# Decay levels of a gated linear attention beside the input projection of a two-block network, a folded Fourier transform, and four PSUM banks in turn

## The chip, the cores and the metric

The kernel runs on one core of a Trainium2 chip, as one launch that computes the whole network. The metric is device time in microseconds (us), the median of the runs of a kernel. The engines are TensorE (PE in the rows, its weight loads PEld), VectorE (DVE), ScalarE (ACT), GpSimd (POOL) and SyncE (SP), which issues the DMAs. Each engine takes its instructions in order, and semaphores tie the engines together.

## The reference, cut to what matters

Two blocks of two layers each over 512 tokens of width 1024, all in float32. The second block has 256 more context tokens in its first layer, so 768 in all. In block 1 each layer is a mixer, a layer norm, a convolutional feed-forward and another layer norm. The change touches mostly the first mixer of block 2:

```
p = h @ w_in                                  # 1024 -> 2064
u_f, q, k, v, r, z = split(p)                 # 512, 256, 256, 512, 512, 16
loga[d] = log_sigmoid(z @ w_gate[d] + b_gate[d]) / 16     # d: forward, backward
# per chunk, for each direction, b = cumsum(loga):
attn[i, j] = sum_d q[i, d] k[j, d] exp(b[i, d] - b[j, d]),  j <= i
o = attn @ v + (q * exp(b)) @ S
S = exp(b_last) * S + (k * exp(b_last - b))^T v
o = (o_f + o_b) * rsqrt(mean(o^2) + eps) * g * silu(r)
f = fft2(u_f, over time and over 128 features of each of 4 groups, ortho).real
y = concat(f, o) @ w_out
```

## The kernel before

Activations lie with features on the 128 partitions and tokens along the free axis. A weight product `pe_product` (line 317) takes a tile of 128 outputs; its weight and its input are each split into a high and a low part of the fast float32 format, so each of the 8 parts of 128 inputs takes three matmuls per token segment (512 latent tokens, and 256 of context where they take part). The order of all tiles is one list; tile g uses weight buffer g % 2. SyncE loads the tile, ScalarE makes its high part (`act_split`, line 287) once product g − 2 is done, VectorE its low part (`dve_split`, line 295), and TensorE multiplies. The product goes to PSUM banks 2(g % 2) and 2(g % 2) + 1, for the context and the latent segment, and may start when tile g − 2 has been taken from there. Where only latent tokens take part, bank 2(g % 2) stays unused. `pe_pair` (line 343) runs the first two tiles of a stage staggered, as their inputs come out of a norm part by part.

In the feed-forward of block 1 (`act_ffn`, `dve_ffn`, `dve_up`) ScalarE takes the middle tap of the convolution from PSUM, VectorE adds the other two (line 1615), and only then is the bank free. Ahead of that, `act_norm` ends with eight scalings of `x` (`act_scaled`, line 1439), which the residual needs later.

The second block's mixer runs in four steps, one after the other on every engine:

- `in2`: 17 tiles (k and q, r, z, v, u by their places in the stacked weight), each copied out by ScalarE (line 355).
- `pe_fourier`: the gates (line 2186) of both directions, with ScalarE and VectorE making log-sigmoid and the running sums (`dve_gl_gates`); the values turned by TensorE transposes (line 2052); then for four groups the feature transform (line 2065), ScalarE's copy of its rows, and the time transform (line 2078) with 4 + 4 row tiles of 128 for latent tokens and 2 + 2 for context.
- the levels: for chunks of 128 tokens, the lower triangle of scores is built from the diagonal and 7 halvings, for two directions: 15 score steps. Step i has arguments by VectorE (`dve_decay_arg`, lines 671 and 672, two halves), an exp by ScalarE (line 678), a multiplication with q and k by VectorE (`dve_decayed`, line 687, two halves), 24 small products by TensorE (`pe_scores`, line 771), and a copy of the wanted places out of PSUM by VectorE (`dve_scores`, line 798). Steps 0, 1, 2, 8 and 9 are "wide" (128 columns a product, three groups of units, the third in the banks of the first); the others "narrow" (64 columns, two groups). Masks for the copies are cast by GpSimd (line 735) from a DMA.
- the tail: keys with their decay turned (line 2284), state products (line 2306) and VectorE's chain of states (line 2491), attention times values (line 2329), q times states (line 2344), a norm per head, then the gate `silu(r)`.

After that comes `out2`, which starts as a pair with the Fourier groups' high and low parts.

## Time and profile before

| what | us |
|---|---|
| median of 3 runs | 2865.52 |
| lowest and highest run | 2852.60, 2868.56 |
| profiled execution | 2854.13 |
| its span | 2852.8 |
| TensorE busy | 2641.2 (93%) |
| VectorE busy | 1745.5 (61%) |
| ScalarE busy | 1083.6 (38%) |

The profile is one execution. Matmuls are pipelined and their ends modelled, so that a busy TensorE need not be at its peak. A float32 matmul outside the weight products leaves two records of each kind. "Granted clock" is the share of full speed that TensorE was allowed. Times in the rows are from the start of the span.

### The profile page before, as it was taken

The page shows a single profiled execution, that of the slowest core. Times are in us where ns is not written, and L with a number is a line of the kernel's source. Part 1 is how long each engine was busy: PE and PEld are TensorE (multiplying, and loading weights), DVE is VectorE, ACT ScalarE, POOL GpSimd, SP SyncE. Part 2 cuts the span into 40 slices and gives each one's busy share as a digit, 9 for nine tenths or more (in the row PEclk, how much of TensorE's full clock was granted, in tenths as well). Part 3 has the DMA queues.
Part 4 walks back from the last instruction along what each step waited for, and adds up shares of the span by engine and source line. Part 5 has one row for each costly group of instructions (what it writes and reads, how often), then busy time and mean ns, then how long its engine had stood idle before and what let it go on. Part 6 is the DMA issues. An engine that isn't in the chain of part 4 may idle for free.

```text
span 2852.8 us, 32720 instructions
## 1 busy us (share of the span) xinstructions
PE 2641.2 (93%) x13412; PEld 2207.7 (77%) x13412; DVE 1745.5 (61%) x2381; ACT 1083.6 (38%) x1472; POOL 37.5 (1%) x38
## 2 busy tenths in 40 slices
PE   5987889999989999899888999999999887999998
PEld 4766768888768888688587788888887666788887
DVE  6786588787778877611595555335533676564464
ACT  2434453233453244422334433213324454443342
POOL 0010000000100000000100000000000000000000
PEclk9986999999999999999859999999999999999999
DMA  8620358755235666231000122211211100233332
GB/s 316 217 81 1 103 165 277 237 177 167 70 101 184 200 201 201 65 112 52 10 1 30 46 67 66 71 57 60 73 64 51 37 29 9 73 97 104 89 105 80
DMA packets 79700, 295.60 MB, mean 104 GB/s; under 512 B 8752, under 2 KB 10416, under 8 KB 79296
## 3 DMA queue, kind: packets, MB, share of 16 engines
q1 hardware_dynamic: 79552, 293.52, 31.9%
q8 instruction: 106, 1.74, 0.2%
q14 instruction: 42, 0.34, 0.0%
HBM read 291.39 MB, written 2.10 MB: 103 GB/s over the span
## 4 chain that ended last, share of the span: by engine, by line
PE 83%; DVE 9%; ACT 4%; issue 1%; POOL 0%; DMA 0%; DVEq 0%; ACTq 0%; SPq 0%
PE ps L317 69%; PE ps L343 3%; PE ps L771 2%; PE ps L2669 1%; PE ps L2078 1%; PE ps L2637 1%; DVE gatt L798 1%; DVE p_lo L2939 1%; DVE w_lo L295 1%; DVE anm L2921 1%; PE ps L1679 1%; DVE h_lo L525 1%; PE ps L1120 1%; ACT h_hi L519 0%; ACT sq L1902 0%
## 5 line engine op out<-in xcount | busy, mean ns | idle before, releaser
L317 PE MATMUL ps<-h_hi,w_hi 128*128 128x512 f32 (+1 forms) x2400 | 807.2, 372 | 24.3 <-DVE conv_u L1615 10.4
L317 PE MATMUL ps<-h_hi,w_lo 128*128 128x512 f32 (+1 forms) x2400 | 798.4, 368 | 0.0
L317 PE MATMUL ps<-h_lo,w_hi 128*128 128x512 f32 (+1 forms) x2400 | 796.7, 367 | 0.0
L295 DVE TENSOR_TENSOR w_lo<-w_raw,w_hi 128x1024 fp32r<-128x1024 f32 (+2 forms) x319 | 413.9, 1298 | 559.8 <-ACT w_hi L287 558.9
L287 ACT ACTIVATE w_hi<-w_raw 128x1024 fp32r<-128x1024 f32 (+2 forms) x319 | 356.7, 1118 | 864.3 <-PE ps L317 833.9
L317 PEld LDWEIGHTS ps<-h_hi,w_hi 128*128 128x128 f32 x2400 | 453.2, 189 | 108.2 <-issue 20.7
L317 PEld LDWEIGHTS ps<-h_lo,w_hi 128*128 128x128 f32 x2400 | 453.6, 189 | 77.3 <-issue 2.9
L317 PEld LDWEIGHTS ps<-h_hi,w_lo 128*128 128x128 f32 x2400 | 452.8, 189 | 75.8
L317 PE MATMUL ps<-g_hi,w_hi 128*128 128x512 f32 (+1 forms) x880 | 295.7, 369 | 0.8 <-DVE w_lo L295 0.8
L317 PE MATMUL ps<-g_lo,w_hi 128*128 128x512 f32 (+1 forms) x880 | 294.8, 368 | 0.0
L317 PE MATMUL ps<-g_hi,w_lo 128*128 128x512 f32 (+1 forms) x880 | 294.8, 368 | 0.0
L439 DVE CUSTOM_DVE_ANT_0 m_raw<-m_raw,c_act,small 128x1024 f32<-128x1024 f32 x179 | 226.3, 1279 | 1.3 <-DMA m_raw<-in_ada_w 1.3
L364 DVE SCALAR_TENSOR_TENSOR x<-ps,mods,x 128x512 f32<-128x512 f32 (+1 forms) x112 | 75.3, 690 | 197.8 <-PE ps L317 190.0
L317 PEld LDWEIGHTS ps<-g_hi,w_hi 128*128 128x128 f32 x880 | 165.3, 188 | 29.6 <-DVE w_lo L295 1.4
L317 PEld LDWEIGHTS ps<-g_lo,w_hi 128*128 128x128 f32 x880 | 165.3, 188 | 28.2 <-issue 0.5
L317 PEld LDWEIGHTS ps<-g_hi,w_lo 128*128 128x128 f32 x880 | 165.3, 188 | 27.8
L1615 DVE SCALAR_TENSOR_TENSOR conv_u<-ps,small,conv_u 128x510 f32<-128x510 f32 (+2 forms) x220 | 148.5, 691 | 3.1
L1571 ACT ACTIVATE g_hi<-gated 128x512 fp32r<-128x512 f32 (+1 forms) x88 | 60.3, 686 | 223.7 <-DVE gated L1628 223.7
L1566 ACT ACTIVATE silu_u<-conv_u 128x512 f32<-128x512 f32 (+1 forms) x88 | 60.4, 687 | 191.7 <-DVE conv_u L1615 191.7
L343 PE MATMUL ps<-h_hi,w_hi 128*128 128x256 f32 (+1 forms) x192 | 66.6, 402 | 59.4 <-DVE w_lo L295 34.6
L1630 DVE TENSOR_TENSOR g_lo<-gated,g_hi 128x512 fp32r<-128x512 f32 (+1 forms) x88 | 66.8, 759 | 66.2 <-ACT g_hi L1571 66.2
L343 PEld LDWEIGHTS ps<-h_hi,w_hi 128*128 128x128 f32 x192 | 37.8, 204 | 76.4 <-issue 52.9
(396 smaller groups left out, 2824.5 us busy)
## 6 DMA issues: line engine op xcount, KB each, us to landing
w_raw<-in_up SPq DMA_DIRECT2D x176, 512.0 KB, 3.6
m_raw<-in_w_mod SPq DMA_DIRECT2D x96, 512.0 KB, 3.7
w_raw<-in_down SPq DMA_DIRECT2D x64, 704.0 KB, 4.1
m_raw<-in_ada_w SPq DMA_DIRECT2D x83, 512.0 KB, 4.7
w_raw<-in_in SPq DMA_DIRECT2D x39, 512.0 KB, 3.7
w_raw<-in_out SPq DMA_DIRECT2D x16, 512.0 KB, 3.6
m_start<-in_ada_w SPq DMA_DIRECT2D x13, 512.0 KB, 12.1
w_raw<-in_qkv SPq DMA_DIRECT2D x12, 512.0 KB, 3.6
```

Of the source, the lines that this page charges most:

```text
L287: act.activation(k.w_hi[s][:, 0:w], k.w_raw[s][:, 0:w], ACT.Copy).then_inc(*k.tick("w_hi", g))
L295: dve.tensor_tensor(k.w_lo[s][:, 0:w], k.w_raw[s][:, 0:w], k.w_hi[s][:, 0:w].bitcast(F32), ALU.subtract).then_inc(*k.tick("w_lo", g))
L317: last = pe.matmul(ps[:, bank, 0:tn], a[:, c, :], b[:, c, t0:t0 + tn], start=c == 0 and n == 0, stop=c == kt - 1 and n == 2)
L343: last = pe.matmul(ps[:, bank, 0:tn], a, b[:, c, t0:t0 + tn], start=c == 0 and n == 0, stop=c == KD - 1 and n == 2)
L364: last = dve.scalar_tensor_tensor(x, k.ps[:, 2 * s + bank, 0:tn], gates[bank], x, ALU.mult, ALU.add)
L439: dve.tensor_tensor_reduce(w, w, k.c_act[:, last, :], 1.0, bias, ALU.mult, ALU.add, column(last)).then_inc(*k.tick("mods", job.key))
L525: k.nc.vector.tensor_tensor(k.h_lo[:, f, ts], value, k.h_hi[:, f, ts].bitcast(F32), ALU.subtract).then_inc(*k.tick("h_lo", key))
L771: last = pe.matmul(out, lhs[rows, cols], right, start=True, stop=True)
L1566: act.activation(f["silu"][:, :], f["conv"][0][:, :], ACT.Silu).then_inc(*k.tick("silu", g))
L1571: act.activation(f["hi"][:, j, :], f["g"][:, :], ACT.Copy).then_inc(*k.tick("g_hi", (block, layer, half, j)))
L1615: last = dve.scalar_tensor_tensor(o, ps[:, bank, lo - d:hi - d], w, o, ALU.mult, ALU.add)
L1630: dve.tensor_tensor(f["lo"][:, j, :], f["g"][:, :], f["hi"][:, j, :].bitcast(F32), ALU.subtract).then_inc(*k.tick("g_lo", key))
```

## The change

**Banks.** For the stages with latent tokens alone (`out1`, the feed-forwards of block 1, the last feed-forward of block 2) tile g uses one bank of (1, 3, 0, 2)[g % 4] and waits for the taking of tile g − 4. **Scalings.** `act_scaled` leaves `act_norm`, and runs one at a tile, from tile 4 of the following up projection. **Order of `in2`.** The tiles are now z, k and q, u, v, r. The gates come inside tile 2 and behind it; the score steps come one after every fifth part, from the fifth part of tile 5 on; the turning of one direction's keys at the third part of tile 16. VectorE's and ScalarE's work for them stands between their splits of the tiles. Buffers lie in other places, and the load of the masks and GpSimd's part come at the start of `in2`. **Fourier.** VectorE folds each group's tokens in `in2` (sum and difference of token t and its mirror), so that the time transform has half of the rows; the tables are half as large, and loaded after the last product of `in2`. High and low halves are made from PSUM directly. The rest is reordered between value turning, keys, states and groups. `silu(r)` and its two table loads stand between the Fourier copies.

```diff
+def in_four(g):
+    return ORDER[g][0] in ("out1", "up00", "down00", "up01", "down01", "up11", "down11")
+def product_bank(g, bank):
+    return (1, 3, 0, 2)[g % 4] if in_four(g) else 2 * (g % 2) + bank
+def bank_release(g):
+    before = g - 4 if in_four(g) else g - 2
+    return (RELEASE[before],) if before >= 0 else ()
...
-    ps = k.ps[:, 2 * s:2 * s + 2, :] if place is None else k.ps[:, place - 1:place + 1, :]
     if 0 in part:
         pe.wait_ge(*k.seen("w_lo", g))
-        for key in free or ((RELEASE[g - 2],) if g >= 2 else ()):
+        for key in free or bank_release(g):
...
+                last = pe.matmul(k.ps[:, product_bank(g, bank) if place is None else place, 0:tn], a[:, c, :], b[:, c, t0:t0 + tn],
...
-    for f in range(KD if split is not None else 0):
-        act_scaled(k, which, f)
...
+            if not half and scaled is not None and 4 <= n < 4 + KD:
+                act_scaled(k, scaled, n - 4)
...
+Z, QK, U, V, R = 0, 1, 5, 9, 13
+LEVEL_STEPS = {4 + 5 * i: i for i in range(2 * LEVELS + 1)}
+KEYS_STEP = 90
...
     sp.wait_ge(*k.seen("h_lo", (("rms", 0), KD - 1)))
-    sp.dma_start(k.tmp[0][0:16, :].rearrange("p (f c) -> p f c", c=P), k.ins["w_gate"]).then_inc(*k.tick("turn_load", "gate", 16))
+    sp.dma_start(k.mean[0:16, :].rearrange("p (f c) -> p f c", c=P), k.ins["w_gate"]).then_inc(*k.tick("turn_load", "gate", 16))
+    sp.dma_start(k.rstd[:, :], k.ins["reset2"]).then_inc(*k.tick("turn_load", "reset2", 16))
+    sp.dma_start(mask_stage(k.gkdt[1], 2), k.ins["masks2"]).then_inc(*k.tick("load", "masks2", 16))
+    sp_tiles(k, BASE["in2"] + 3, 14)
+    sp.wait_ge(*k.seen("product", BASE["in2"] + 16))
     sp.dma_start(k.feat[:, :], k.ins["dft_f"]).then_inc(*k.tick("load", "dft_f", 16))
-    sp.dma_start(k.dlat[:, :, :, :], k.ins["dft_lat"]).then_inc(*k.tick("load", "dft_lat", 16))
-    sp.dma_start(k.dctx[:, :, :, :], k.ins["dft_ctx"]).then_inc(*k.tick("load", "dft", 16))
-    sp.dma_start(k.greset, k.ins["reset2"]).then_inc(*k.tick("load", "reset2", 16))
-    sp_tiles(k, BASE["in2"] + 3, 14)
+    sp.dma_start(k.dctx[:, :, :, :], k.ins["dft_ctx"]).then_inc(*k.tick("load", "dft_ctx", 16))
+    sp.dma_start(k.dlat[:, :, :, :], k.ins["dft_lat"]).then_inc(*k.tick("load", "dft", 16))
...
 def pe_in2(k):
-    pe_pair(k, BASE["in2"], TALL, k.h_hi, k.h_lo, rms_ready(0))
-    for n in range(2, 17):
-        pe_product(k, BASE["in2"] + n, TALL, k.h_hi, k.h_lo)
+    g0 = BASE["in2"]
+    pe_pair(k, g0, TALL, k.h_hi, k.h_lo, rms_ready(0))
+    pe_product(k, g0 + 2, TALL, k.h_hi, k.h_lo, part=range(0, 4))
+    pe_gl_gates(k, 0)
+    pe_product(k, g0 + 2, TALL, k.h_hi, k.h_lo, part=range(4, KD))
+    pe_gl_gates(k, 1)
+    for n in range(3, U):
+        pe_product(k, g0 + n, TALL, k.h_hi, k.h_lo)
+    for n in range(U, 17):
+        for c in range(KD):
+            pe_product(k, g0 + n, TALL, k.h_hi, k.h_lo, part=range(c, c + 1))
+            step = (n - U) * KD + c
+            if step in LEVEL_STEPS:
+                pe_gl_scores(k, LEVEL_STEPS[step])
+            if step == KEYS_STEP:
+                pe_gl_keys(k, 1)
 def act_in2(k):
-    for n in range(17):
-        if n:
+    for n in range(1, 18):
+        if n < 17:
             act_split(k, BASE["in2"] + n + 1)
-        if n:
-            act_keep_in2(k, n - 1)
-    act_keep_in2(k, 16)
-def act_keep_in2(k, n):
-    act_keep(k, BASE["in2"] + n, k.z2[:, n, :] if n < 9 else k.more[:, n - 9, :], TALL)
+        act_keep(k, BASE["in2"] + n - 1, in2_place(k, n - 1), TALL)
+        if n == 2:
+            act_gl_biased(k, 0)
+        if n == 3:
+            act_gl_exp(k, 0)
+            act_gl_log(k, 0)
+            act_gl_biased(k, 1)
+        if n == 4:
+            act_gl_exp(k, 1)
+            act_gl_log(k, 1)
+        if n == U:
+            act_decay(k, "g", 0, gl_combs(k)[0], 1.0 / 16.0)
+        for i in levels_beside(n):
+            if i + 1 < len(GL_STEPS):
+                act_decay(k, "g", i + 1, gl_combs(k)[(i + 1) % 3], 1.0 / 16.0)
+        if n == 15:
+            act_gl_decays(k)
+        if n == 17:
+            act_gl_turned(k, 1)
...
 def dve_in2(k):
     for n in range(1, 17):
         dve_split(k, BASE["in2"] + n + 1)
+        if n == 2:
+            dve_gl_abs(k, 0)
+        if n == 3:
+            dve_gl_gates(k, 0)
+            dve_gl_abs(k, 1)
+        if n == 4:
+            dve_gl_scaled(k)
+            dve_gl_gates(k, 1)
+        if n == U:
+            dve_gl_first(k)
+        for i in levels_beside(n):
+            dve_gl_level(k, i)
+        if U + 2 <= n < U + 6:
+            dve_fo_fold(k, n - U - 2)
+        if n == 15:
+            dve_gl_decays(k)
+def dve_fo_fold(k, g):
+    dve, u = k.nc.vector, k.fu[:, g, :]
+    dve.wait_ge(*k.seen("kept", BASE["in2"] + U + g))
+    for n, (t0, tn, _) in enumerate(FOLDED):
+        half = tn // 2
+        right = u[:, t0 + half + 1:t0 + tn]
+        dve.tensor_tensor(right, right, u[:, t0 + half - 1:t0:-1], ALU.subtract).then_inc(*k.tick("unfolded", (g, n)))
+    for n, (t0, tn, _) in enumerate(FOLDED):
+        half = tn // 2
+        left = u[:, t0 + 1:t0 + half]
+        dve.wait_ge(*k.seen("unfolded", (g, n)))
+        last = dve.scalar_tensor_tensor(left, left, 2.0, u[:, t0 + tn - 1:t0 + half:-1], ALU.mult, ALU.add)
+    last.then_inc(*k.tick("folded", g))
...
-    pe_gl_gates(k, 0)
     pe_fo_values(k)
+    pe_gl_keys(k, 0)
+    pe_gl_add(k, 1)
     pe_fo_features(k, 0)
-    pe_gl_gates(k, 1)
-    for g in range(4):
-        if g + 1 < 4:
-            pe_fo_features(k, g + 1)
-        pe_fo_time(k, g)
+    pe_fo_features(k, 1)
+    pe_fo_time(k, 0)
+    pe_fo_features(k, 2)
+    pe_fo_time(k, 1)
+    pe_gl_add(k, 0)
+    pe_fo_features(k, 3)
+    pe_fo_time(k, 2)
+    pe_fo_time(k, 3)
...
+    pe.wait_ge(*k.seen("kept", BASE["in2"] + V + 3))
+    pe.wait_ge(*k.seen("turned_out", ("gkd", 1, 2)))
+    pe.wait_ge(*k.seen("att", ("g", steps, len(score_groups(GL_STEPS, steps, 24)) - 1)))
...
-    for t in range(TALL // P):
-        last = pe.matmul(k.ps[:, 4 + t // 2, (t % 2) * 256:(t % 2) * 256 + 256], k.more[:, 4 + g, t * P:(t + 1) * P], k.feat[:, :],
-                         start=True, stop=True)
+    pe.wait_ge(*k.seen("folded", g))
+    for t0, tn, odd in FOLDED:
+        for j in range(tn // 2 // P):
+            t = odd // P + j
+            place = lambda rows, part: k.ps[rows, t // 2, (t % 2) * 256 + part * P:(t % 2) * 256 + (part + 1) * P]
+            middle = t0 + tn // 2
+            pe.matmul(place(slice(0, P), 0), u[:, t0 + j * P:t0 + (j + 1) * P], k.feat[:, 0:P], start=True, stop=True)
+            last = pe.matmul(place(slice(0, P), 1), u[:, middle + j * P:middle + (j + 1) * P], k.feat[:, P:2 * P], start=True, stop=True)
+            if j == 0:
+                last = pe.matmul(place(slice(0, 1), 1), u[:, middle:middle + 1], k.feat[:, 0:P], start=True, stop=True)
...
-    for t0, tn, bank in segments(TALL):
-        basis, nt = (k.dctx, k.dlat)[bank], tn // P
+    if g >= 2:
+        pe.wait_ge(*k.seen("h_lo", ("fourier", g - 2)))
+    for (t0, tn, bank), (_, _, odd) in zip(segments(TALL), FOLDED):
+        basis, nt = (k.dctx, k.dlat)[bank], tn // 2 // P
         for part in range(2):
             for t in range(nt):
-                last = pe.matmul(k.ps[:, 2 * (g % 2) + bank, 0:tn], a[:, t0 // P + t, part * P:(part + 1) * P], basis[:, part, t, :],
+                last = pe.matmul(k.ps[:, fo_bank(g, bank), 0:tn], a[:, odd // P + t, part * P:(part + 1) * P], basis[:, part, t, :],
...
     act_fo_rows(k, 0)
-    act_gl_biased(k, 1)
-    for d in range(2):
-        act_gl_exp(k, d)
     act_fo_rows(k, 1)
-    for d in range(2):
-        act_gl_log(k, d)
-    for g in range(4):
-        act_fo_out(k, g)
-        if g + 2 < 4:
-            act_fo_rows(k, g + 2)
+    act_fo_high(k, 0)
+    act_fo_rows(k, 2)
+    act_fo_high(k, 1)
+    act_fo_rows(k, 3)
+    act.activation(k.silu(0), k.silu(0), ACT.Silu).then_inc(*k.tick("gl_silu", 0))
+    act.activation(k.silus[:, :, :], k.silus[:, :, :], ACT.Silu).then_inc(*k.tick("gl_silu", 1))
+    act_tables(k)
+    act_fo_high(k, 2)
+    act_fo_high(k, 3)
...
+def act_fo_high(k, g):
+    act = k.nc.scalar
     act.wait_ge(*k.seen("fourier_t", g))
-    if g:
-        act.wait_ge(*k.seen("h_lo", ("fourier", g - 1)))
-    act.activation(k.rstd[:, 0:CTX], k.ps[:, b0, 0:CTX], ACT.Copy)
-    act.activation(k.rstd[:, CTX:TALL], k.ps[:, b0 + 1, 0:LAT], ACT.Copy).then_inc(*k.tick("fourier_out", g))
-    act.wait_ge(*k.seen("fourier_out", g))
-    act.activation(k.h_hi[:, g, :], k.rstd[:, :], ACT.Copy).then_inc(*k.tick("h_hi", ("fourier", g)))
-def dve_fourier(k):
-    dve, q = k.nc.vector, gl_views(k)[0]
-    dve.tensor_scalar(q, q, 0.125, None, ALU.mult).then_inc(*k.tick("gl_q"))
-    for d in range(2):
-        dve_gl_abs(k, d)
-    for d in range(2):
-        dve_gl_gates(k, d)
-    for g in range(4):
-        dve_low(k, "fourier", g, slice(0, TALL), k.rstd[:, :])
+    for t0, tn, bank in segments(TALL):
+        last = act.activation(k.h_hi[:, g, t0:t0 + tn], k.ps[:, fo_bank(g, bank), 0:tn], ACT.Copy)
+    last.then_inc(*k.tick("h_hi", ("fourier", g)))
...
+def dve_fo_low(k, g):
+    dve = k.nc.vector
+    dve.wait_ge(*k.seen("h_hi", ("fourier", g)))
+    for t0, tn, bank in segments(TALL):
+        last = dve.tensor_tensor(k.h_lo[:, g, t0:t0 + tn], k.ps[:, fo_bank(g, bank), 0:tn], k.h_hi[:, g, t0:t0 + tn].bitcast(F32), ALU.subtract)
+    last.then_inc(*k.tick("h_lo", ("fourier", g)))
...
-    pool.wait_ge(*k.seen("fourier_t", 3))
+    pool.wait_ge(*k.seen("product", BASE["in2"] - 1))
...
-    if d == 0:
-        act.preload_act_table_set("natural_log")
...
+def pe_gl_scores(k, i):
+    pe = k.nc.tensor
+    if i == 0:
+        q, _, _, doubled, _ = gl_views(k)
+        pe.wait_ge(*k.seen("gl_k2"))
+        pe_scores(k, "g", 0, doubled, q, GL_UNITS, GL_STEPS)
+    else:
+        c = gl_combs(k)[(i - 1) % 3]
+        pe.wait_ge(*k.seen("decayed", ("g", i - 1)))
+        pe_scores(k, "g", i, c, c, GL_UNITS, GL_STEPS)
...
+    pe.wait_ge(*(k.seen("turned_out", ("gkd", 0, 2)) if d else k.seen("state", ("g", 1, NC2 - 1))))
...
+        pe.wait_ge(*k.seen("h_lo", ("fourier", 3)))
...
+def dve_gl_first(k):
+    dve, (_, kk, (e0, e1), doubled, _) = k.nc.vector, gl_views(k)
+    dve.wait_ge(*k.seen("mask_g", len(GL_STEPS)))
+    dve_decay_arg(k, "g", 0, e0, gl_combs(k)[0], 0, False)
+    dve.wait_ge(*k.seen("kept", BASE["in2"] + QK + 3))
+    dve.wait_ge(*k.seen("gl_q"))
+    dve.tensor_scalar(doubled, kk, 2.0, None, ALU.mult).then_inc(*k.tick("gl_k2"))
+def dve_gl_level(k, i):
+    dve, (q, kk, (e0, e1), _, _), combs, steps = k.nc.vector, gl_views(k), gl_combs(k), len(GL_STEPS)
+    if i + 1 < steps:
+        d, level = GL_STEPS[i + 1]
+        if i + 1 == LEVELS:
+            dve.wait_ge(*k.seen("gl_back", 1))
+        if i + 1 >= 2:
+            dve.wait_ge(*k.seen("scored", ("g", i - 1, len(score_groups(GL_STEPS, i - 1, 24)) - 1)))
+        dve_decay_arg(k, "g", i + 1, (e0, e1)[d], combs[(i + 1) % 3], level, d == 1)
+    if i < steps:
+        d, level = GL_STEPS[i]
+        dve_decayed(k, "g", i, combs[i % 3], level, d == 1, q, kk)
+    if i == 0:
+        dve.wait_ge(*k.seen("zeroed", "g"))
+    dve_scores(k, "g", i, k.gatt, k.gmasks, 24, GL_STEPS)
...
     dve_gl_states(k, 1)
-    dve.wait_ge(*k.seen("q_decay", ("g", 1)))
-    dve.tensor_tensor(e1, e1, q, ALU.mult).then_inc(*k.tick("q_decayed", "g"))
-    dve.wait_ge(*k.seen("q_decayed", "g"))
+    dve_fo_low(k, 0)
+    dve_fo_low(k, 1)
     dve_gl_states(k, 0)
+    dve_fo_low(k, 2)
+    dve_fo_low(k, 3)
```

## Rows read from the trace of the kernel before

**Rows 1.** The page, parts 1 and 4: busy time and share by engine; the chain of waits by engine.

```profile
PE 2641.2 (93%) x13412; PEld 2207.7 (77%) x13412; DVE 1745.5 (61%) x2381; ACT 1083.6 (38%) x1472; POOL 37.5 (1%) x38
...
PE 83%; DVE 9%; ACT 4%; issue 1%; POOL 0%; DMA 0%; DVEq 0%; ACTq 0%; SPq 0%
```

**Rows 2.** Busy time by stage: stretch, length, engines (instructions), granted clock, DMA share, GB/s.

```profile
1217.20:1344.46 127.26, 127.23 (x721) 110.12 (x719) 19.26 (x16) 27.35 (x45) 0.00 (x0) 1.00 0.27 91
1344.46:1402.00 57.54, 55.24 (x184) 33.92 (x184) 18.65 (x14) 25.64 (x33) 0.00 (x0) 0.97 0.00 0
1402.00:1500.00 98.00, 74.72 (x720) 71.87 (x720) 88.04 (x94) 30.68 (x23) 13.51 (x16) 0.59 0.03 8
1500.00:1538.35 38.35, 27.54 (x250) 22.55 (x251) 22.56 (x33) 21.75 (x29) 0.00 (x0) 0.88 0.05 15
```

**Rows 3.** Timelines after a pair: start, us, engine, line, operation, tiles, shape, [idle <-releaser].

```profile
377.47 5.74 ACT L1439 ACTIVATE x<-x,coef 128x512 f32<-128x512 f32 x8
...
387.00 0.77 PE L317 MATMUL ps<-h_hi,w_hi 128*128 128x512 f32 x1 [4.93 <-DVE conv_u L1615]
...
823.08 0.77 PE L317 MATMUL ps<-h_hi,w_hi 128*128 128x512 f32 x1 [3.61 <-DVE conv_u L1615]
...
2488.06 1.23 DVE L295 TENSOR_TENSOR w_lo<-w_raw,w_hi 128x1024 fp32r<-128x1024 f32 x1 [2.23 <-ACT w_hi L287]
...
2490.88 0.47 PE L317 MATMUL ps<-h_hi,w_hi 128*128 128x512 f32 x1 [1.28 <-DVE conv_u L1615]
```

**Rows 4.** Granted clock in four stretches, columns as in rows 2.

```profile
386.00:392.40 6.40, 5.40 (x13) 4.27 (x14) 5.67 (x10) 2.32 (x4) 0.00 (x0) 0.50 0.72 235
823.10:826.50 3.40, 3.40 (x9) 2.71 (x10) 3.40 (x6) 1.45 (x2) 0.00 (x0) 0.54 0.54 147
...
1441.00:1457.00 16.00, 16.00 (x152) 15.95 (x150) 16.00 (x19) 4.64 (x4) 0.00 (x0) 0.50 0.01 2
1472.00:1475.00 3.00, 3.00 (x58) 3.00 (x58) 2.93 (x4) 0.00 (x0) 0.00 (x0) 1.00 0.00 0
```

**Rows 5.** TensorE's timeline in the levels: wide scores, then narrow ones.

```profile
1428.64 1.16 PE L771 MATMUL ps<-spare 64*128 64x128 f32 x16 [1.15 <-DVE gatt L798]
...
1472.71 2.79 PE L771 MATMUL ps<-gkdt 64*128 64x64 f32 x48
```

**Rows 6.** Groups by line and shape, 1180 to 1620: count, busy us, mean ns, idle before.

```profile
L295 DVE TENSOR_TENSOR w_lo<-w_raw,w_hi 128x1024 fp32r<-128x1024 f32 x26 | 31.9, 1225 | 114.2 <-ACT w_hi L287 114.2
L798 DVE COPY_PREDICATED gatt<-gmasks,ps 128x1024 f32<-128x1024 uint8 x25 | 31.4, 1276 | 7.7 <-PE ps L771 7.5
...
L678 ACT ACTIVATE gkdt<-gkdt 128x1536 f32<-128x1536 f32 x5 | 7.4, 1485 | 19.3 <-DVE gkdt L672 19.3
...
L798 DVE COPY_PREDICATED gatt<-gmasks,ps 128x512 f32<-128x512 uint8 x10 | 7.1, 706 | 0.5 <-PE ps L771 0.5
...
L2230 DVE TENSOR_TENSOR_SCAN gtop<-greset,spare 128x768 f32<-128x768 f32 x4 | 6.8, 1744 | 0.1
...
L671 DVE TENSOR_TENSOR gkdt<-gtop 128x768 f32<-128x768 f32 x5 | 4.7, 945 | 0.0
```

**Rows 7.** Chain of waits, 1344 to 1538: start, us, engine, tile, line, records.

```profile
1345.48 2.83 PE ps L2186 x8
...
1351.08 1.24 PE ps L2052 x6
...
1362.39 8.59 PE ps L2078 x24
1370.98 2.59 PE ps L2065 x12
...
1520.73 2.50 PE ps L2344 x40
1523.23 1.98 PE ps L2329 x16
```

**Rows 8.** DMA issues, 1190 to 1420: line, engine, count, KB, us to landing.

```profile
dft_lat<-in_dft_lat SPq DMA_DIRECT2D x1, 2048.0 KB, 9.2
```

More of the change, by code:

```diff
@@ L342, in pe_pair @@
                     t0 -= TALL - b.shape[2]
-                    last = pe.matmul(ps[:, bank, 0:tn], a, b[:, c, t0:t0 + tn], start=c == 0 and n == 0, stop=c == KD - 1 and n == 2)
+                    last = pe.matmul(k.ps[:, product_bank(t, bank), 0:tn], a, b[:, c, t0:t0 + tn], start=c == 0 and n == 0, stop=c == KD - 1 and n == 2)
             if c == KD - 1:
@@ L363, in dve_add @@
         x = k.x[:, f, t0:t0 + tn]
-        last = dve.scalar_tensor_tensor(x, k.ps[:, 2 * s + bank, 0:tn], gates[bank], x, ALU.mult, ALU.add)
+        last = dve.scalar_tensor_tensor(x, k.ps[:, product_bank(g, bank), 0:tn], gates[bank], x, ALU.mult, ALU.add)
     last.then_inc(*k.tick("taken", g))
```

238 lines of the change are left out of this document (108 added, 130 removed).

## The prediction

> **What bounds the kernel now.** I read the shares of the page first, then busy time by stage, then the places where TensorE waited, and last the chain of waits through the gap found. TensorE is the bound: busy 93% of the span, 83% of the chain [rows 1]. Inside a run of weight products there is nothing to hide: in the second input projection (`in2`) 15 tiles take 127.26 us with TensorE busy throughout at full clock, 8.48 us a tile and 1.06 for each of its 8 parts [rows 2]. So only two things help: shorter gaps between products, and less TensorE time outside them. From the end of `in2` at 1344.46 to the start of `out2` at 1538.35 lie 193.9 us without a weight product: the Fourier stage (57.5), the decay levels (98.0, VectorE busy 88.04, mean granted clock 0.59) and the tail of the gated attention (38.4). VectorE sets the pace of the levels, and in `in2` it is busy 19.26 of 127.26 us [rows 2]. That is the room the change uses.
>
> **1. Four banks in turn, and the scaling moved.** After the first two tiles of an up projection TensorE waits 4.93, 3.61 and 1.28 us, each time for the convolution that frees the bank of the tile two before. In block 1 ScalarE first ran its eight scalings (5.74 us), with the next weight's split queued behind them. At 2490.88 there is no scaling: VectorE's part of the split began at 2488.06 and took 1.23, over at 2489.3 as the pair ended, so the whole 1.28 is the bank [rows 3]. With four banks that wait goes; with the scalings behind tile 4, so does the late split. What is late next is the weight itself: 0.2 us at each, so 9.8 − 0.6 = 9.2. The gaps also cost clock: after the first, 6.4 us are granted 0.50 (3.2 us of work lost), after the second 3.4 us at 0.54 (1.6) [rows 4]. Sum 14, bounds 0 (should the weight be as late as the bank) and 15. Elsewhere the banks give nothing, as tiles follow without a gap. The sixteen scalings (0.72 each) lie one to a tile on a ScalarE with little else; without that cover each would cost its 0.72.
>
> **2. TensorE work that moves into `in2`.** Fifteen score levels. Five are wide: 48 records, of which 16 take 1.16 us at full clock, so 3.5. Ten are narrow: 48 records take 2.79 with a short overlap, so 2.75 [rows 5]. 5 × 3.5 + 10 × 2.75 = 45. Two gate products at 2.83 are 5.7; twelve key transposes at 1.24/6 are 2.5 [rows 7]. About 17 switches between kinds of product at some 0.2 each, an estimate from the 0.14 us between the last copy and the gates (1345.35 to 1345.48): 3. Sum 56.
>
> **3. What TensorE waits for in `in2`.** VectorE's loop for level i is: two half-width subtractions for level i+1, two multiplications of that shape for level i (each 0.945), then the copies out of PSUM, 0.71 + 1.28 for a narrow level, 3 × 1.28 for a wide one [rows 6]: 5.8 and 7.6 us. Each tile adds a weight split of 1.23 [rows 6], and four tiles a fold that the trace lacks; it is four passes over halves of 768 columns, so under 4 × 0.945, and I take 1.5. TensorE returns with a level after five parts (5.3) and its own scores, every 8.1 to 8.8 us. So a narrow level is covered, by a little. A wide one is not: its third group of scores reuses the banks of the first, and VectorE's first copy stands behind subtractions and multiplications.
> Walked on the times of before. Tile 2 starts at 1217.2, gates of direction 0 at 1221.5; tile 3 starts at 1231.3 behind both gate products. ScalarE does the exp and log (1.485 each [rows 6]) after tile 2's split and copy, at 1233.6; VectorE's scans (two of 1.744 [rows 6]) with the passes around them end at 1239.2, direction 1 follows through ScalarE and ends at 1252.4; split, first argument and doubled keys at 1256.5. TensorE is at level 0 at 1253.6, four tiles and five parts on: wait 3.0. Level 0's third group waits 3.9 for two subtractions, two multiplications and a copy; level 1 waits 4.2, as the split of tile 7 comes between; level 2 0.2, levels 8 and 9, behind folds and splits, 1.5 and 3.1. Sum 16. While TensorE stands there, the rest of its tile and through it the next splits stand behind it; that is in the walk. After four of these waits I take 1.6 us of lost clock, as in rows 4: 6. Waits and clock are 22, bounds 0 and 96 (rival C).
> The other queues: SP has only 1 MB (gate weights, reset row, masks) in front of the next weights here, where before 3.1 MB stood. GpSimd's clearing and mask casts begin earlier and lie beside the first tiles; VectorE needs the last mask at 1253.7. Two table loads for log and exp fall away on ScalarE, beside products.
> `in2` grows by 56 + 22 = 78.
>
> **4. What is left behind `in2`.** A group's time transform took 8.59 (24 records); with half the rows 4.3. A feature transform was 2.59; now 16 records of 128 columns at 1.98/16 = 0.124 are 2.0 [rows 7]. The new chain, in us after the last product: that tile kept (1.0, as 1344.46 to 1345.48) and three copies of turned keys at an estimated 0.6, 2.8; four value transposes at 1.24 [rows 7], 7.8; last copy, keys of direction 0 with ScalarE's three copies, 11.3; state products of direction 1, the last waiting for VectorE's third state, 13.5; features 0 and 1 with one copy between, 18.4; time 0, features 2, time 1, 29; state products of direction 0, which wait for VectorE's low halves of groups 0 and 1 and then three states, 32.8; features 3, times 2 and 3, 43.4; high and low halves of the last group, which the values now wait for, 45.7; values of two heads, 24 × 0.124, 48.7; then what ran from 1520.73 (first product with the states [rows 7]) to 1538.35, unchanged, 17.6: 66.3. The first 13 us hold little but transposes and waits. At half clock their TensorE time (5 and 2.5) would double at most; I add 5, and 2 for hand-overs: 73, bounds 66 and 85. The DFT tables are now fetched only after the last product: 1.4 MB that are needed 13.5 us later, where 2 MB took 9.2 [rows 8]. Hidden; a landing after 13.5 would cost the excess.
> The Trainium skill (TensorE: Matmul & The Clock Gate, Part 4: PE-mode transpose) says that transposes do not count as busy for the clock: by that the first 13 us run wholly at half clock, and the stage is 76 in place of 73. The Trainium skill (ScalarE: Activation LUTs, What ACT_TABLE_LOAD costs) gives a switch of tables 2.66 us as an estimate, with a drain; two switches stand before the high halves of groups 2 and 3, and by it these would be 1.7 later than above.
>
> **5. The sum.** The profiled execution took 2854.1 (span 2852.8). 2854.1 − 14 − 193.9 + 73 + 78 = 2797. It lies 11.4 under the median of the three runs, which spread over 16; I add half of that for a median: **2803**.
>
> **Rivals.**
> A. *Hidden wholly.* VectorE gets ahead and no level waits. For it: VectorE's 19.26 of 127.26 us. Against it: its order, in which the first copy of a wide level is behind four passes. It gives 22 back: 2781.
> B. *The clock falls at every level.* For it: from 1441 to 1457 TensorE was busy all the time with narrow scores and stood at 0.50. Against it: from 1472 to 1475 scores ran at 1.00 [rows 4], and in `in2` five dense parts lie between. In full: a narrow level at 16.0/152 = 0.105 us a record is 5.05, +2.3 for ten; a wide one doubled, +3.5 for five; 1.6 behind each of 15: 64, less the 6 in the sum: 2861. At every second level: 2832. The same page of the Trainium skill (HAM oscillation) describes such a fall once in every turn of a loop with pauses; which it is here, only the run can tell.
> C. *Slower: VectorE and TensorE alternate.* If every level holds TensorE until VectorE's loop is through, the waits are 10 × 5.8 + 5 × 7.6 = 96 in place of 16: 2883. It decides from 78 us of waits, where the gain over 2865.5 is gone. For it: one queue per engine, with splits, folds and gates on the same VectorE. Against it: each argument is made a whole level ahead, so the multiplications never wait for ScalarE.
> D. *The banks do nothing*, since the weight is as late as the bank: 14 less gained, 2817. Against it is 2490.88.
>
> **Chances.** Forecast 0.52, A 0.13, B 0.18 (a quarter of it in full), C 0.06, D 0.11. The range takes in A, D and B at every second level, with the bounds behind `in2`: 2776 to 2838; outside are B in full and C. A measurement of this kernel tells 0.5% (14 us) from no change. Faster by more: 0.90; within: 0.05 (B in full); slower: 0.05 (C).
>
> **What would show it.** No bank wait before the third tile of those up projections. Score products after every fifth part of `in2`, with TensorE waits over 1 us only before level 0 and in wide levels, 16 us in all. `in2` 78 us longer (wrong under 56 or over 100), 73 us from its end to `out2`, time transforms of 4.3. Clock of 1.0 in `in2` but behind those waits. The prediction fails if narrow levels wait (C), if scores in `in2` run at 0.5 (B), or if the part behind `in2` shows a wait for a DMA.

## The result and the profile after

The changed kernel took 2792.84 us (median of four runs, 2789.01 to 2794.49), the kernel before 2865.82 (2852.6 to 2868.56) beside it: a ratio of 0.975 [0.972, 0.978], 73 us less. Forecast were 2803 and a gain of 62.5. The kernel before was run 26 times more beside the first experiments, with a median of 2857.05; against that the gain is 64 us. The profiled execution took 2792.61 (span 2791.3) where that of before took 2854.13 (span 2852.8), so the two traces differ by 61.5.

The page after: busy time and share by engine; TensorE's granted clock in 40 slices of the span; the chain of waits by engine.

```profile
PE 2599.2 (93%) x13380; PEld 2169.6 (78%) x13380; DVE 1749.7 (63%) x2401; ACT 1072.7 (38%) x1467; POOL 34.6 (1%) x38
...
PEclk9986999999999999999999999999999998999999
...
PE 85%; DVE 8%; ACT 4%; issue 1%; DMA 1%; POOL 0%; SPq 0%; ACTq 0%; DVEq 0%
```

TensorE's busy time fell by 42.0 [rows 1]. About 17 of that are the halved time transforms (4 × 4.3). Most of the rest is clock, for nearly the same products: the scores moved from a stretch at 0.59 clock [rows 2] to stretches near 1.00. The other 19.5 of the 61.5 were idle time.

The stages, columns as in rows 2: `in2` from its pair of tiles on; from there to `out2`; two stretches inside `in2`, one of narrow levels, one behind the third group of level 0; and the stretch that showed the first bank gap and its half clock before [rows 4].

```profile
1182.75:1407.49 224.74, 208.06 (x1564) 178.74 (x1564) 146.47 (x155) 73.98 (x93) 8.34 (x15) 0.95 0.14 43
1407.49:1475.33 67.84, 54.62 (x373) 37.41 (x374) 17.34 (x36) 33.45 (x48) 0.00 (x0) 0.99 0.09 30
1284.53:1320.30 35.77, 35.77 (x361) 32.13 (x362) 28.16 (x37) 12.85 (x14) 0.00 (x0) 1.00 0.13 41
1250.00:1262.00 12.00, 9.38 (x72) 7.97 (x68) 7.19 (x8) 3.30 (x4) 0.00 (x0) 0.86 0.00 0
386.00:392.40 6.40, 6.40 (x30) 5.31 (x29) 5.68 (x9) 2.25 (x3) 0.00 (x0) 1.00 0.87 291
```

| part | predicted | by the two traces |
|---|---|---|
| all up to `in2`, the banks and the scaling | −14 | −16.0 (1198.70 − 1182.75), 14.2 of it behind the first pair of the FFN |
| `in2` | +78 | +79.0 (224.74 − 145.76) |
| end of `in2` to `out2` | −120.9 (73 − 193.9) | −126.1 (67.84 − 193.89) |
| behind it | 0 | +1.5 |
| sum | −57 | −61.5 |

The third of the bank places lies behind `out2`, so of the 14 forecast about 1 belongs in the row "behind it". It came: from one norm to the next the last feed-forward took 371.06 in place of 372.56. The row is up all the same, since other parts were longer, among them one whose code is unchanged (300.2 in place of 298.0; 298.1 to 301.1 in the other traces).

The banks, on the timeline after the first pair (start, us, engine, line, operation, tiles):

```profile
378.87 1.06 ACT L307 ACTIVATE w_hi<-w_raw 128x1024 fp32r<-128x1024 f32 x1 [3.09 <-PE ps L361]
...
379.96 1.23 DVE L315 TENSOR_TENSOR w_lo<-w_raw,w_hi 128x1024 fp32r<-128x1024 f32 x1 [2.25 <-ACT w_hi L307]
...
381.33 0.41 PE L336 MATMUL ps<-h_hi,w_hi 128*128 128x512 f32 x1
```

The split is over at 381.2, just before TensorE arrives at 381.33: no gap where 4.93 stood [rows 3], none either at the other two places, and the 6.4 us that ran at 0.50 [rows 4] are at 1.00.

TensorE's timeline in `in2`, the operations of the gated attention alone (last bracket: idle before, and the releaser). Lines 790 and 2300 are 771 and 2186 of before.

```profile
1209.97 4.77 PE L2300 MATMUL ps<-gate_low,mean 16*128 16x256 f32 x8 [4.29 <-DMA rstd<-in_reset]
...
1220.35 2.84 PE L2300 MATMUL ps<-gate_low,mean 16*128 16x256 f32 x8
...
1249.23 2.06 PE L790 MATMUL ps<-gla_qk,gcomb 64*128 64x128 f32 x32 [2.07 <-DVE gcomb L2551]
1253.90 1.16 PE L790 MATMUL ps<-gla_qk,gcomb 64*128 64x128 f32 x16 [2.62 <-DVE gatt L817]
...
1267.10 1.16 PE L790 MATMUL ps<-gkdt 64*128 64x128 f32 x16 [3.08 <-DVE gatt L817]
...
1277.87 1.16 PE L790 MATMUL ps<-gcomb 64*128 64x128 f32 x16 [0.61 <-DVE gatt L817]
1284.45 2.90 PE L790 MATMUL ps<-gcomb 64*128 64x64 f32 x48
...
1328.53 1.16 PE L790 MATMUL ps<-gcomb 64*128 64x128 f32 x16 [0.89 <-DVE gatt L817]
...
1340.17 1.87 PE L790 MATMUL ps<-gcomb 64*128 64x128 f32 x16 [3.08 <-DVE gatt L817]
```

Read the brackets: one wait for a DMA, one for the doubled keys (line 2551), and five before the third group of a wide level, for VectorE's copy (line 817). No narrow level has one. They add up to 16.6 us. Where the first comes from is shown by the chain of waits there (start, us, what):

```profile
1201.61 1.07 ACT w_hi L307
...
1202.70 1.24 DVE w_lo L315
...
1203.96 0.33 SPq L297
...
1204.33 0.43 SPq L2024
...
1204.81 5.12 DMA rstd<-in_reset
```

SyncE's queue holds the load of the weight of tile 5 (line 297), and it may only start when the split of tile 3 has freed its buffer at 1203.94. The gate weights and the reset row stand behind it; the row needs 5.12 us to land.

### The profile page after: what moved, and what is told of

The parts are those of the page before. It is cut to its first block, busy times and chain, and to the rows that moved or that the text cites. A ratio compares the mean times of both kernels' runs of the same rounds, so it can differ in the third digit from the quotient of the medians.

```text
span 2791.3 us, 32675 instructions
## 1 busy us (share of the span) xinstructions
PE 2599.2 (93%) x13380; PEld 2169.6 (78%) x13380; DVE 1749.7 (63%) x2401; ACT 1072.7 (38%) x1467; POOL 34.6 (1%) x38
## 4 chain that ended last, share of the span: by engine, by line
PE 85%; DVE 8%; ACT 4%; issue 1%; DMA 1%; POOL 0%; SPq 0%; ACTq 0%; DVEq 0%
PE ps L336 70%; PE ps L361 4%; PE ps L790 3%; PE ps L2805 1%; PE ps L2773 1%; DVE w_lo L315 1%; DVE p_lo L3075 1%; PE ps L2202 1%; DVE anm L3057 1%; PE ps L1139 1%; PE ps L1699 1%; DVE h_lo L543 0%; PE ps L2786 0%; DVE x L1503 0%; ACT h_hi L537 0%
## 5 line engine op out<-in xcount | busy, mean ns | idle before, releaser
L336 PEld LDWEIGHTS ps<-g_hi,w_hi 128*128 128x128 f32 x880 | 165.3, 188 | 29.5 <-DVE w_lo L315 1.4
```

The source lines that it names most:

```text
L336: last = pe.matmul(k.ps[:, product_bank(g, bank) if place is None else place, 0:tn], a[:, c, :], b[:, c, t0:t0 + tn], start=c == 0 and n = ...
```

## The experiments

The kernel before ran beside each group of experiments: medians 2857.05 (26 runs), 2857.68 and 2861.4 (9 each). Its runs spread over up to 20 us, so each result below is the ratio to it, and small steps between changed kernels are read by their medians and their traces.

**Part 1 alone, and its halves.** To the kernel before were added the banks (first three lines; all readers follow `product_bank`), the moved scaling (the rest), or both.

```diff
+def product_bank(g, bank):
+    return (1, 3, 0, 2)[g % 4] if in_four(g) else 2 * (g % 2) + bank
...
+    before = g - 4 if in_four(g) else g - 2
...
-    for f in range(KD if split is not None else 0):
-        act_scaled(k, which, f)
...
+            if not half and scaled is not None and 4 <= n < 4 + KD:
+                act_scaled(k, scaled, n - 4)
```

Both:

> The kernel before with part 1 alone: four banks in turn, and the eight scalings moved behind tile 4. Theory: the gaps of 4.93, 3.61 and 1.28 us go to under 0.3 each, and with them the 6.4 and 3.4 us at half clock, so 14 us less (13 to 15) in the span, nothing from the second block's mixer. Rival (the weight is as late as the bank): the gaps stay at 2 us or more, under 6 us gained.

Banks alone:

> The kernel before with four banks in turn, the scalings left where they were. Theory: in block 1 TensorE now waits for the weight, whose split stands behind the scalings: gaps of some 3.3 and 2.0 us in place of 4.93 and 3.61 (the low half was over 1.6 us ahead of the bank), none at the last feed-forward; the clock still falls; 4.5 us gained. Rival (the banks are the whole cause): gaps under 0.5 and 14 gained.

Scaling alone:

> The kernel before with the scalings moved, two tiles' banks in turn as before. Theory: the block 1 gaps shrink to what the feed-forward without scalings shows, 1.3 to 1.6 us, and the clock no longer falls; the last one stays at 1.28; 10 us gained. Rival (the banks are the whole cause): the gaps stay above 3 us.

Measured: both 2841.67 (10 runs), ratio 0.994 [0.992, 0.996], 15.4 less; banks alone 2856.56 (10 runs), 1.000 [0.997, 1.002]; scaling alone 2849.38 (10 runs), 0.997 [0.995, 1.000], 7.7 less. The gaps in block 0, of banks alone and then of scaling alone:

```profile
384.14 0.50 PE L329 MATMUL ps<-h_hi,w_hi 128*128 128x512 f32 x1 [2.24 <-DVE w_lo L308]
...
817.42 0.50 PE L329 MATMUL ps<-h_hi,w_hi 128*128 128x512 f32 x1 [2.12 <-DVE w_lo L308]
```

```profile
385.27 0.47 PE L317 MATMUL ps<-h_hi,w_hi 128*128 128x512 f32 x1 [1.28 <-DVE conv_u L1615]
...
814.38 0.47 PE L317 MATMUL ps<-h_hi,w_hi 128*128 128x512 f32 x1 [1.36 <-DVE conv_u L1615]
```

Two causes lay one behind the other. With the scalings moved and the banks as before, a wait of 1.3 us for the bank remains; with the banks changed and the scalings left, a wait of 2.2 us for the late split remains; with both edits, nothing. The rival that the banks do nothing falls by these rows, and the 14 of the sum is held by the 15.4.

The interval of the banks' time reaches from 7 us less to 5 more, so the medians don't settle their share. The traces do, by the time from one norm's `sum,ones` product to the next around the three places (two of these stretches differ by up to 1.6 us between traces of kernels that do the same there):

| kernel | first | second | third | less in all |
|---|---|---|---|---|
| before | 382.32 | 310.84 | 372.56 | |
| banks alone | 379.77 | 309.26 | 371.07 | 5.6 |
| scaling alone | 376.89 | 305.01 | 372.56 | 11.3 |
| both | 375.63 | 303.30 | 371.06 | 15.7 |

The banks alone were expected to give 4.5, the scaling alone 10.

**The levels, all behind `in2`.** The changed kernel with its levels and the keys of direction 1 in one piece after the last tile; ScalarE's and VectorE's work for the levels, and the decays of keys and queries, go there with them. Of the edit, TensorE's part:

```diff
-            if step in LEVEL_STEPS:
-                pe_gl_scores(k, LEVEL_STEPS[step])
-            if step == KEYS_STEP:
-                pe_gl_keys(k, 1)
+    for i in range(len(GL_STEPS) + 1):
+        pe_gl_scores(k, i)
+    pe_gl_keys(k, 1)
```

> The changed kernel with all 15 score levels behind the last tile of the input projection in place of beside it; gates, fold, banks and the order behind it stay. Theory (the gain is the overlap): the projection gets 60 us shorter than in the changed kernel (45 of scores, 16 of waits and their clock), the levels then take 95 as in the kernel before, and the decays of keys and queries lie open for 8: 43 us slower than the changed kernel, about 2836. Rival (the gain is in the new order of the Fourier part and the fold): within 15 us of the changed kernel.

Measured: 2829.03 (5 runs), ratio 0.991 [0.988, 0.994]: 36 us of the gain come from placing the levels between products, where 43 were expected. By the traces `in2` is 68 us shorter than in the changed kernel (156.6 and 224.7), where 60 were expected, and the part behind it 103 longer. Its levels, columns as in rows 2:

```profile
1343.50:1435.67 92.17, 73.55 (x690) 70.69 (x688) 81.18 (x87) 19.76 (x15) 0.00 (x0) 0.57 0.04 15
```

VectorE is busy 88% of it and the clock is at 0.57, as in the kernel before [rows 2]. So it is the placing, and no other edit, that ends both the waiting for VectorE and the half clock.

**The reset row ahead of a weight.** The waits of the changed kernel were then taken away one by one.

```diff
-    sp_tiles(k, BASE["in2"], 3)
+    sp_tiles(k, BASE["in2"], 2)
-    sp_tiles(k, BASE["in2"] + 3, 14)
+    sp_tiles(k, BASE["in2"] + 2, 15)
```

> The changed kernel with the DMAs of the gates' weights, the reset row and the masks issued before the load of tile 5 instead of behind it. In the changed kernel TensorE waited 4.3 us for the reset row in tile 2, and the gates then took 4.8 in place of 2.8. Theory (SyncE's queue order delays the row, as the load in front waits for a low half): that wait goes, and 6 us are gained; some of it, up to 4, can be given back at level 0, where VectorE's chain from the gates is late by then. Rival (the row's own landing time of 5 us is the cause): under 1 us gained.

Measured: 2788.51 (4 runs), ratio 0.976 [0.974, 0.978], 4.3 less than the changed kernel, where 6 were expected. The gates start without a wait; level 0 waits a little longer:

```profile
1242.66 2.06 PE L790 MATMUL ps<-gla_qk,gcomb 64*128 64x128 f32 x32 [2.33 <-DVE gcomb L2551]
1247.34 1.64 PE L790 MATMUL ps<-gla_qk,gcomb 64*128 64x128 f32 x16 [2.62 <-DVE gatt L817]
```

Columns as in rows 2, the stretch with both gates, and all of `in2`:

```profile
1190.00:1242.00 52.00, 50.34 (x272) 41.48 (x270) 29.43 (x27) 23.19 (x35) 9.33 (x15) 1.00 0.21 66
1185.10:1402.17 217.07, 204.54 (x1564) 177.15 (x1564) 146.73 (x155) 73.95 (x92) 9.33 (x15) 0.96 0.15 45
```

The row's place in SyncE's queue was the cause. `in2` is 7.6 us shorter than the 224.7 of the changed kernel: 4.29 of waiting, and the clock, which no longer falls at the gates (both take 2.84) nor in the products behind them. What it frees is mostly kept: 0.26 us of it comes back as a wait at level 0. Elsewhere this trace is 3.9 us longer, 2.3 of it before `in2`, where the code is the same; the medians show 4.3 of the gain.

**Copies first in the wide levels.**

```diff
+    if is_wide(GL_STEPS, i):
+        dve_scores(k, "g", i, k.gatt, k.gmasks, 24, GL_STEPS)
     (subtractions for level i+1, multiplications for level i)
-    dve_scores(k, "g", i, k.gatt, k.gmasks, 24, GL_STEPS)
+    if not is_wide(GL_STEPS, i):
+        dve_scores(k, "g", i, k.gatt, k.gmasks, 24, GL_STEPS)
```

> The changed kernel where VectorE does a wide level's copies before the next argument and the multiplications. Theory (the third group of a wide level waits because the copies stand behind four passes): the waits inside the wide levels, 2.6, 3.1, 0.6, 0.9 and 3.1 us, fall to 0.3 each, and the clock lost behind three of them, 4 us, comes back; some new waits of 1 us at the level after a wide one: 11 us gained, bounds 6 and 13. Rival (the wait is the copy itself): under 3 gained.

Measured: 2783.85 (4 runs), ratio 0.974 [0.972, 0.976], 9.0 less. Three of its five waits, and the clock of the stretch in which level 0's third group stands:

```profile
1254.46 1.16 PE L790 MATMUL ps<-gla_qk,gcomb 64*128 64x128 f32 x16 [0.60 <-DVE gatt L817]
1263.69 1.16 PE L790 MATMUL ps<-gkdt 64*128 64x128 f32 x16 [0.68 <-DVE gatt L817]
1272.93 1.16 PE L790 MATMUL ps<-gcomb 64*128 64x128 f32 x16 [0.60 <-DVE gatt L817]
```

```profile
1250.00:1262.00 12.00, 9.59 (x96) 8.46 (x98) 9.79 (x11) 4.67 (x5) 0.00 (x0) 1.00 0.14 44
```

The five waits are 3.3 us (0.60, 0.68, 0.60, 0.60, 0.79) in place of 10.3, and the clock that fell to 0.86 behind the first of them stays at 1.00. `in2` is 213.8 us long, 10.9 less than in the changed kernel: 7.0 of waiting, and for the other 3.9 the trace offers the clock. The expectation was 11; the median shows 9.0 of it. VectorE's order was the cause, not its load.

**Copies first in every level.** Should the narrow levels then wait, since the next level's argument is late? The same edit with `if True:` in place of the test.

> The changed kernel with the copies first in every level, narrow ones too. Theory (only the third group of a wide level needs it; in a narrow level the multiplications come later instead): behind a narrow level's last scores VectorE now needs 1.3 + 3.8 = 5.1 us, and 1.2 more with a split or 1.0 with a fold, before the next level's scores may start, against 5.4 of products; waits of about 0.9 us at six or seven levels, 6 us slower than with the copies first in wide levels alone (2783.9), near 2790. Rival (copies first is better everywhere): no slower than 2784.

Measured: 2782.03 (5 runs, 2779.83 to 2795.07), ratio 0.974 [0.971, 0.977]: the theory was wrong, nothing was lost against 2783.85. VectorE's timeline behind the scores of the first narrow level, and TensorE's next scores:

```profile
1280.31 1.26 DVE L817 COPY_PREDICATED gatt<-gmasks,ps 128x1024 f32<-128x1024 uint8 x1 [0.87 <-PE ps L790]
1281.47 0.94 DVE L689 TENSOR_TENSOR gcomb<-gla_b 128x768 f32<-128x768 f32 x1
1282.34 0.95 DVE L690 TENSOR_TENSOR gcomb<-gla_b 128x768 f32<-128x768 f32 x1
1283.20 1.82 DVE L705 TENSOR_TENSOR gkdt<-gkdt,gla_qk 128x768 f32<-128x768 f32 x2
1284.94 0.62 DVE L2117 TENSOR_TENSOR fourier_u<-fourier_u 128x127 f32<-128x127 f32 x2
1285.48 0.61 DVE L2122 SCALAR_TENSOR_TENSOR fourier_u<-fourier_u 128x127 f32<-128x127 f32 x2
1286.01 1.22 DVE L315 TENSOR_TENSOR w_lo<-w_raw,w_hi 128x1024 fp32r<-128x1024 f32 x1
...
1285.59 2.90 PE L790 MATMUL ps<-gkdt 64*128 64x64 f32 x48
```

The multiplications end at 1285.0, and TensorE comes to the scores that need them at 1285.59, after five parts: covered, with 0.6 us to spare. The fold and the split stand behind them, where nothing waits for them.

**How much room narrow levels have.** The changed kernel with a level after every fourth part.

```diff
-LEVEL_STEPS = {4 + 5 * i: i for i in range(2 * LEVELS + 1)}
+LEVEL_STEPS = {4 + 4 * i: i for i in range(2 * LEVELS + 1)}
```

> The changed kernel with a level after every fourth part of the projection in place of every fifth. Theory (VectorE's loop of 5.8 us for a narrow level, 7 to 8.5 with a split or a fold, is covered by 8.2 of TensorE): at 4.3 + 2.8 = 7.1 us the cover is gone where a split or fold comes between, so narrow levels wait 1 us in about half of the cases and wide ones 1 more: 10 us slower. Rival (VectorE has room left): within 2 us.

Measured: 2799.58 (5 runs), ratio 0.980 [0.978, 0.982], 6.7 more than the changed kernel. The third groups of the wide levels wait 1.71, 4.10, 0.60, 2.22 and 4.10, 12.7 in place of 10.3, and no narrow level waits. `in2` is 5.8 us longer (230.5); these waits are 2.4 of it, and what the rest is was not taken apart. The theory was half right: closer levels cost time, but a narrow one has cover to spare. The rows of the last experiment show why: operations on VectorE that last 0.95 start 0.87 apart, so the loop is 4 × 0.87 + 0.70 + 1.16 = 5.3 and not 5.8, and TensorE comes back after 4 × 1.06 + 2.85 = 7.1.

**The time transform twice.** Is TensorE the bound behind `in2`, or would a chain through ScalarE and VectorE set the end anyway? The products are added twice into the bank, so the transform's output is doubled.

```diff
+        for again in range(2):
             (the loops over part and t, into the same bank)
```

> The changed kernel with each group's time transform run twice into the same bank (so the transform's output is doubled): TensorE's work as without the fold. Theory: all of it lies open, 4 x 4.3 = 17 us slower. Rival (VectorE's and ScalarE's chain of states and low halves sets the pace there): under 10 us slower.

Measured: 2810.46 (4 runs), ratio 0.984 [0.982, 0.986], 17.6 more; the added products are worth 4 × 4.3 = 17.2. By the traces the part behind `in2` is longer by 18.6 than in the first trace of the changed kernel and by 17.2 than in its second. The transform lies on the path with its whole length, so folding it in half was worth what its TensorE time says.

**The changed kernel once more.**

> The changed kernel itself, beside the three variants of it. Theory and rival alike: within 0.2% of its first time, 2792.8; its runs lie within 6 us of each other, where those of the kernel before spread over 20.

Measured: 2797.87 (5 runs, 2792.19 to 2801.56), ratio 0.978 [0.976, 0.980]; its median is 0.18% over the first, and its spread is 9 us, where 6 were expected. Steps of under about 5 us between changed kernels rest on their traces, not on their medians.

**All three together.** The reset row early, copies first in wide levels, and the doubled keys ahead of the first argument:

```diff
-    dve.wait_ge(*k.seen("mask_g", len(GL_STEPS)))
-    dve_decay_arg(k, "g", 0, e0, gl_combs(k)[0], 0, False)
     dve.tensor_scalar(doubled, kk, 2.0, None, ALU.mult).then_inc(*k.tick("gl_k2"))
+    dve.wait_ge(*k.seen("mask_g", len(GL_STEPS)))
+    dve_decay_arg(k, "g", 0, e0, gl_combs(k)[0], 0, False)
```

> The changed kernel with three edits: copies first in wide levels, the DMAs of the reset row and masks ahead of tile 5's load, and the doubled keys before the first argument. Theory (three waits on different chains): gains of 9, 4.3 and, for the third, 1.7 of the 2.3 us before level 0 add up, 15 us under the changed kernel, 2778. Rival (they overlap, since an earlier gate product meets the same VectorE chain at level 0): at best 10 us under, 2783.

Measured: 2774.30 (5 runs), ratio 0.970 [0.968, 0.973]; 18.5 under the changed kernel's first median, 23.6 under the one beside it. The first two gains add up: `in2` is 203.7 us long, 21.0 less than in the changed kernel, where the two edits by themselves gave 7.6 and 10.9. The third edit was not run by itself; the wait before level 0 is 0.60. And the same with each level three parts later (`{7 + 5 * i: ...}`):

> The kernel tuned with all levels three parts later (the first behind the eighth part of tile 5). Theory: the rest of the wait before level 0, 0.6 us, goes, and nothing else changes: 0 to 1 us gained on tuned. Rival (levels meet tile ends and splits at other places, so the small waits move): 2 us or more either way.

Measured: 2773.78 (4 runs), ratio 0.970 [0.968, 0.972]: no difference beyond its scatter, though neither the gates nor level 0 wait at their start (0.85 and 0.60 before); the first waits of TensorE in `in2` are now these:

```profile
1245.71 1.16 PE L790 MATMUL ps<-gla_qk,gcomb 64*128 64x128 f32 x16 [0.60 <-DVE gatt L817]
1254.95 1.16 PE L790 MATMUL ps<-gkdt 64*128 64x128 f32 x16 [0.60 <-DVE gatt L817]
```

These two beat both kernels, by 3% and by 0.7%.

## Why the prediction was right

**The banks and the scaling: right.** 14 forecast; 15.7 by the traces of before and after (14.2 in block 1, 1.5 at the third place), 15.4 by the experiment. The reading that made it was that of one place without a scaling [rows 3], which split the wait into its two causes; both single edits left just the waits that this reading names.

**`in2`: right in sum, by errors that cancel.**

| term | predicted | measured |
|---|---|---|
| scores | 45 | 44.3 (5 × 3.17 + 10 × 2.85) |
| gates at full clock | 5.7 | 5.5 |
| twelve transposes of keys | 2.5 | 1.3 |
| switches | 3 | 1.5 (what is left) |
| waits | 16 | 16.6 |
| lost clock | 6 | 9.8 |
| sum | 78 | 79.0 |

The step that failed is the sentence on SyncE, that it has only 1 MB in front of the next weights. It counted what the row delays, not what delays the row: a weight load that waits for its buffer stood before it, and TensorE waited 4.29 us and ran the gates at half clock (4.77 and not 2.77). Its price is 4.3 us by the medians of the experiment and 7.6 by the length of `in2` in the traces. So the 16.6 of waits are 12.3 for VectorE, where 16 were forecast, and 4.3 for a DMA, where none was; that they meet the 16 is luck. The hand-made walk of VectorE was late by a little nearly everywhere: level 0 was to wait 3.0 and waited 2.07; the third groups 3.9, 4.2, 0.2, 1.5, 3.1 and waited 2.62, 3.08, 0.61, 0.89, 3.08. The fold was taken as 1.5 and took about 1.1, and each product began a little earlier on VectorE than the walk had it. Lost clock is larger, 9.8 and not 6, since two falls at the gates were not in the sum; with the reset row early both were absent, so they belong to the same failed step: 2.0 in the first gate product, 3.0 in the dense products behind the two (12 records each from 1214.66 to 1218.18 and from 1224.27 to 1227.92, at full clock 2.1); behind the three longest waits of wide levels another 4.1, and 0.7 in the last group.

**"A narrow level is covered, by a little": covered, but by more.** A level after every fourth part, and the copies ahead of the multiplications, both left narrow levels without a wait. The prediction set the loop of 5.8 against each return of TensorE, with a split or a fold on top. The loop is 5.3, a split comes once in eight parts, and what is late in one level is caught up in the next.

**Behind `in2`: the walk right, the margin not needed.** The marks, in us after the last product, forecast and measured: state products of direction 1 done 13.5 and 12.5; two groups transformed 29 and 29.5; state products of direction 0 done 32.8 and 33.3; last transform 43.4 and 44.4; values of two heads 48.7 and 49.4; the end 66.3 and 67.8. The 5 us for half clock and the 2 for hand-overs did not come, so 73 was 67.8. The rows show why:

```profile
1409.93 1.50 PE L2162 MATMUL ps<-ident,gla_v 128*128 128x128 f32 x12 [2.48 <-issue]
1411.68 1.58 PE L2162 MATMUL ps<-ident,gla_v 128*128 128x128 f32 x12 [0.25 <-ACT gtop L2212]
```

Twelve transposes took 1.50 us and not 2 × 1.24 [rows 7]. The row that gave the price stood at a fallen clock, as two stretches of the trace of before show:

```profile
1348.22:1350.89 2.67, 2.67 (x13) 2.27 (x12) 0.53 (x1) 2.56 (x5) 0.00 (x0) 0.54 0.00 0
1351.08:1352.32 1.24, 1.24 (x8) 1.24 (x9) 1.04 (x1) 0.66 (x1) 0.00 (x0) 0.69 0.00 0
```

So the forecast paid for slow transposes twice, once in the 1.24 and once in the 5 us; the same price made the keys 2.5 in place of 1.3.

The whole stretch had a clock of 0.99 in this trace, which is in part luck. In the second trace of the changed kernel, and in six of the seven traces of its variants that keep the levels in `in2`, the 24 transposes of values took 4.48 to 4.57 us behind the same wait of 2.48, at half clock for up to 3.4 of them. The row of that second trace, then two stretches of it, columns as in rows 2:

```profile
1408.48 4.57 PE L2162 MATMUL ps<-ident,gla_v 128*128 128x128 f32 x24 [2.48 <-issue]
```

```profile
1408.48:1411.89 3.41, 3.40 (x17) 3.39 (x18) 0.00 (x0) 1.39 (x2) 0.00 (x0) 0.52 0.83 326
1411.95:1413.05 1.10, 1.10 (x9) 0.68 (x7) 0.00 (x0) 0.96 (x2) 0.00 (x0) 1.00 0.00 0
```

That is 1.2 of the 1.4 us by which the stage was longer there. The Trainium skill (TensorE: Matmul & The Clock Gate, Part 4: PE-mode transpose) says that transposes do not count as busy; by that all of these would have run at half clock and the stage would have been 76. The traces do not bear that out: in the first one the transposes ran at 1.00 throughout, and in the second one the clock was back at 1.00 behind 3.4 us of nothing but transposes. The two table loads took 1.28 us each, with at most 0.02 us idle on ScalarE before and behind each. The Trainium skill (ScalarE: Activation LUTs, What ACT_TABLE_LOAD costs) has 2.66 a switch, 1.28 for the load and 1.38 for a drain: the load agrees, the drain does not show here. No wait for a DMA stands in this stretch.

**The rivals.** B, a clock that falls at every level: in the narrow levels TensorE ran 35.77 us without a pause at 1.00, so it is wrong; in the first trace, behind the pair, it fell only around the gates and behind the waits of 2.62, 3.08 and 3.08 in wide levels (0.86 in the stretch with the first). C, alternation: the waits were 16.6 and not 96. It is close to what happens when the levels lie behind the products, as bunched they took 92.17. A, hidden wholly: also wrong, but near at hand; with three edits of order most of the waits went.

**The size.** By the traces the forecast was 4.4 short of the gain; the other 6 us are what was added because the profiled execution before lay under its median. The changed kernel's profiled execution lay at its median, and nothing needed adding. The median that the 6 was taken from was itself high: 2865.5 of three runs, where 26 later ones gave 2857.05. Against those the gain is 64, and the 62.5 forecast fits it closely, but that is luck too: the forecast time was 10 us too long, and the median before was 8.5 too high. The three parts, each by its experiment (36 for placing the levels, 15.4 for banks and scaling, 17.6 for half of the time transforms), add up to 69; the gates' place, the hand-overs and the order behind `in2` were not tried by themselves.

## What to carry to other kernels

When work of a slow engine is laid beside dense products, walk the slow engine's queue in order: what costs is not its load but which of its instructions stands in front of the copy that frees a bank, and putting that copy first took away 7 of 16.6 us of waits, and made the stage 10.9 us shorter in the traces. For every small load that a moved step needs, look at what is ahead of it in the DMA-issuing queue, not only at what comes behind it. Where one wait has two candidates, find a place in the trace where only one of them is present. Before a row's duration is used as a price, look up the clock it was taken at.
